# A long fused block: the merged rows split inside the last branch's panels, the convolution's low part three steps later

## The reference, cut to what matters

```
proj = h @ w_in
u_f, u_sc, u_qkv, z, b_logit, a_logit, gate_logit = split(proj)
y_f  = fourier_mix(u_f) @ w_fourier                      # branch 0
y_sc = short_conv_mix(u_sc, sconv_w) @ w_sconv_out       # branch 1: b * conv3(c * h)
y_dn = deltanet_branch(u_qkv, z, ...) @ w_dn_out         # branch 2: gated delta rule
merged = gates[0] * y_f + gates[1] * y_sc + gates[2] * y_dn
return merged @ w_out
```

## Time and profile before

| | |
|---|---|
| median of three runs | 1087.94 us |
| profiled execution, its own time | 1087.07 us |
| its span in the trace | 1085.3 us |
| mean granted TensorE clock | 0.97 of full |
| busy: TensorE, GpSimd, VectorE, ScalarE | 94%, 70%, 51%, 43% |

### The profile page before, as it was taken

One profiled execution on the slowest core, in us unless ns is written; L12 is line 12 of the kernel. 1 busy time (PEld: TensorE's weight loads), 2 busy tenths in 40 slices (PEclk: granted clock), 3 DMA queues, 4 the chain that ended last, 5 costly groups with the idle time before them and its releaser, 6 DMA issues.

```text
span 1085.3 us, 21538 instructions
## 1 busy us (share of the span) xinstructions
PE 1023.1 (94%) x8142; PEld 995.9 (92%) x8142; DVE 549.1 (51%) x1020; ACT 468.7 (43%) x698; POOL 762.6 (70%) x599
## 2 busy tenths in 40 slices
PE   7999999989899999998999899989999889999996
PEld 6899899989899999997898789989999879999995
DVE  4316994455444443335695463445654764445324
ACT  6243224454355444434546434423235364444441
POOL 2496666647859888996578734646629739999994
PEclk9999999999989999998999899989999889999998
DMA  9363333433526555664353122434225526656662
GB/s 351 106 194 117 117 117 117 136 98 117 194 82 184 173 181 159 181 178 152 117 169 107 57 62 94 120 115 126 90 79 172 188 69 194 193 179 185 178 182 70
DMA packets 48297, 154.60 MB, mean 142 GB/s; under 512 B 6028, under 2 KB 11156, under 8 KB 48232
## 3 DMA queue, kind: packets, MB, share of 16 engines
q1 hardware_dynamic: 46080, 151.31, 44.6%
q10 hardware_dynamic: 2152, 2.38, 0.6%
HBM read 151.57 MB, written 2.10 MB: 142 GB/s over the span
## 4 chain that ended last, share of the span: by engine, by line
PE 76%; DVE 12%; issue 4%; POOL 4%; ACT 3%; DMA 0%; SPq 0%; DVEq 0%; ACTq 0%; POOLq 0%
PE panel L1517 59%; PE panel L1561 3%; POOL wlo L591 2%; PE aux L1653 1%; PE panel L1604 1%; DVE qkv L1246 1%; DVE qkv L1251 1%; PE panel L1592 1%; DVE q L1154 1%; DVE s L1133 1%; DVE qkv L1242 1%; DVE k L1155 1%; PE aux L1875 1%; PE aux L1847 1%; PE aux L1838 1%
## 5 line engine op out<-in xcount | busy, mean ns | idle before, releaser
L591 POOL TENSOR_TENSOR wlo<-raw,whi 128x512 fp32r<-128x512 f32 x552 | 733.5, 1360 | 301.2 <-ACT whi L679 299.9
L1517 PE MATMUL panel<-xh,whi 128*128 128x256 f32 (+1 forms) x1504 | 443.5, 295 | 14.5 <-DVE xl L985 9.9
L1517 PE MATMUL panel<-xh,wlo 128*128 128x256 f32 (+1 forms) x1504 | 431.3, 287 | 0.0
L1517 PE MATMUL panel<-xl,whi 128*128 128x256 f32 (+1 forms) x1504 | 430.7, 286 | 0.0
L679 ACT ACTIVATE whi<-raw 128x1024 fp32r<-128x1024 f32 x276 | 286.5, 1053 | 175.0 <-PE panel L1517 152.2
L1517 PEld LDWEIGHTS panel<-xh,whi 128*128 128x128 f32 x1504 | 288.3, 192 | 19.3 <-issue 11.5
L1517 PEld LDWEIGHTS panel<-xl,whi 128*128 128x128 f32 x1504 | 287.4, 191 | 1.6
L1517 PEld LDWEIGHTS panel<-xh,wlo 128*128 128x128 f32 x1504 | 288.0, 191 | 0.0
L1517 PE MATMUL panel<-hh,whi 128*128 128x272 f32 (+1 forms) x352 | 100.1, 284 | 0.0
L1517 PE MATMUL panel<-hh,wlo 128*128 128x272 f32 (+1 forms) x352 | 99.9, 284 | 0.0
L1517 PE MATMUL panel<-hl,whi 128*128 128x272 f32 (+1 forms) x352 | 99.8, 284 | 0.0
(11 more groups left out here) (285 smaller groups left out, 1495.0 us busy)
## 6 DMA issues: line engine op xcount, KB each, us to landing
raw<-in_panels SPq DMA_DIRECT2D x228, 512.0 KB, 3.5
raw<-in_down SPq DMA_DIRECT2D x32, 448.0 KB, 3.3
raw<-in_down SPq DMA_DIRECT2D x16, 512.0 KB, 3.5
memk<-in_mem_panels SPq DMA_DIRECT2D x4, 512.0 KB, 7.4
memv<-in_mem_panels SPq DMA_DIRECT2D x4, 512.0 KB, 13.2
memx<-in_mem SPq DMA_DIRECT2D x4, 256.0 KB, 5.2
h<-in_x SPq DMA_DIRECT2D x1, 1024.0 KB, 8.0
spill<-h ACTq DMA_DIRECT2D x1, 1024.0 KB, 4.7
```

The costliest lines, as they stand in the source:

```text
L591: ins = nc.gpsimd.tensor_tensor(wlo[:, slot, half], raw[:, slot, half], whi[:, slot, half].bitcast(f32), ALU.subtract)
L1517: ins = M(bank[:, 0:w], wt[:, slot, P * t:P * t + P], x[:, kk, c0:c0 + w], start=first and m == 0 and n == 0, stop=last and m == len(pairs ...
```

## The change

Three things are changed. The merged rows get buffers of their own, `mgh` and `mgl`, in the space of `vt` and `kt` of the delta rule. Their high parts are made by ScalarE at the steps ("branch", 2, i), behind the wait for `mg_ready`, and their low parts by VectorE at the same steps, one tile behind (the last one after the loop). And a step ("sconv_low", t) three places behind ("sconv", t, 2) takes over VectorE's `yl`.

```diff
+    for i in range(4):
+        steps.insert(steps.index(("sconv", i, 2)) + 3, ("sconv_low", i))
     return steps
...
+        mgh = at("mgh", ar + 6528, [P, KT, ROWS], f32r)
+        mgl = at("mgl", ar + 8576, [P, KT, ROWS], f32r)
...
+                if kind == "branch" and step[1] == 2:
+                    act.wait_ge(mg_ready, 8 + i + 1)
+                    A(mgh[:, i, :], mg[:, i, :], ACT.Copy).then_inc(mg_high, 1)
...
             act.dma_start(h[:, :, META:LEN], a["spill"]).then_inc(h_back, 16)
-            out_wait(MIX_OUT[("gate", 2, 7)][0])
-            for kk in range(KT):
-                act.wait_ge(mg_ready, 8 + kk + 1)
-                if kk == 0:
-                    out_wait(MIX_OUT[("branch", 2, 7)][0])
-                A(xh[:, kk, 0:ROWS], mg[:, kk, :], ACT.Copy).then_inc(mg_high, 1)
...
+            def merged_low(kk):
+                dve.wait_ge(mg_high, kk + 1)
+                TT(mgl[:, kk, :], mg[:, kk, :], mgh[:, kk, :].bitcast(f32), ALU.subtract).then_inc(mg_low, 1)
...
                         TT(mg[:, i, :], mg[:, i, :], gt[:, g % 2, :], ALU.add).then_inc(mg_ready, 1)
+                        if step[1] == 2 and i:
+                            merged_low(i - 1)
...
                         TT(y, y, sc[:, t % 2, 0, META:LEN], ALU.mult).then_inc(yc_ready, 1)
-                        dve.wait_ge(y_high, 4 + t + 1)
-                        TT(yl[:, t, :], y, yh[:, t, :].bitcast(f32), ALU.subtract).then_inc(y_low, 1)
+                if kind == "sconv_low":
+                    dve.wait_ge(y_high, 4 + i + 1)
+                    TT(yl[:, i, :], cc[:, i % 2, 1, 0:ROWS], yh[:, i, :].bitcast(f32), ALU.subtract).then_inc(y_low, 1)
...
-            for kk in range(KT):
-                dve.wait_ge(mg_high, kk + 1)
-                TT(xl[:, kk, 0:ROWS], mg[:, kk, :], xh[:, kk, 0:ROWS].bitcast(f32), ALU.subtract).then_inc(mg_low, 1)
+            merged_low(KT - 1)
...
-                output(OUT2_O + i, OUT2_P + i, xh, xl, ROWS, each=(lambda kk: pe.wait_ge(mg_low, kk + 1)) if i == 0 else None)
+                output(OUT2_O + i, OUT2_P + i, mgh, mgl, ROWS, each=(lambda kk: pe.wait_ge(mg_low, kk + 1)) if i == 0 else None)
```

## The result

The changed kernel took 1079.74 us in the median of five runs (1078.5 to 1082.48), the kernel before 1087.07 in five (1086.77 to 1089.46): a ratio of 0.9936, 95% interval 0.9921 to 0.9951. A second comparison, 12 runs against 35, gave 1080.17 against 1085.83: 0.9949 (0.9935 to 0.9963), so 4 to 7 us. The forecast was 1081.3.

What follows compares the result with a forecast made beforehand. TensorE, busy 94% of the span, bounds the kernel, so only its stalls and slow-clock stretches can be won. Split 5.2 plus convolution 1.2 gives 6.4 us: 1080.7 for the profiled execution, 1081.3 taken, range 1079.2 to 1085.4.

Steps and rivals of the forecast that it cites:

- the prediction's own signs of being wrong: Granted clock 0.50 behind the output-pass stall, TensorE waiting for `wlo` between panels 194 and 203, or low parts over 2.3 us.
- The convolution's part: Delta rule: low part three steps later brings `aoff` earlier at two stalls, saving 0.45 and 0.75, together 1.2 us.
- The split: Mixer's end: merged rows split tile by tile inside the branch steps let the output panels start earlier, saving 5.2 us.
- low part 6 costs 0.41: Mixer's end: VectorE's low part of merged tile 6 takes 0.41 us, with GpSimd at the end of its queue.
- the two variants: The split saves 5.4 us, or 5.05 if longer `wlo` end GpSimd's queue 0.9 us later, about 847.1; 5.2 taken.
- Rival 1: Output passes: the clock falls again behind the shorter stall, 6.8 us at half speed costing 3.3 us; 1084.6 us, chance 0.26.
- Rival 2: Mixer's end: VectorE loses the port more than once, operations cost 2.68 us each; slower, 1089.5 to 1092.7 us, chance 0.06.
- What ScalarE's waits hold up: Branch steps: panel 200's weights' high part ends 2.0 to 4.2 us later, just hidden; nothing taken, up to 1 us lost.
- The sum: Whole kernel: 5.2 + 1.2 = 6.4 us saved, 1080.7 for the profiled execution; 1081.3 taken, chance 0.55.

Runs made afterwards that it cites:

- `aoff` ahead: The changed kernel with `aoff` of the second level's unit 1 made right behind unit 0, ahead of the convolution's five operations: 1072.89 us, ratio 0.9882 against before.
- split alone: Against the changed kernel, only the merged rows are split tile by tile; the convolution's low part stays in its step: 1082.28 us, ratio 0.9966 against before.
- convolution alone: Against the kernel before, only the convolution's low part is made three steps later; merged rows are split at the end: 1084.64 us, ratio 0.9994.
- the changed kernel's repeat: The changed kernel run and profiled once more with no edit: 1080.17 us, ratio 0.9949 against before.
- both edits: The changed kernel with unit 1's `aoff` made ahead of the convolution and the first two output passes interleaved: 1072.23 us, ratio 0.9877 against before.

## Why the prediction was right

*The place and the kind of gain.* Right. TensorE's stall behind the last branch matmul went from 3.5 us to 2.36 plus 0.18 (2.47 and 0.30 between starts, less one step each), and the time moved the way that was forecast. Not all of the mechanism came as forecast: one of the prediction's own signs of being wrong, a granted clock of 0.50 behind the stall, is there in the changed kernel's profile (844.8 to 848.2) and in its repeat. The other two, a wait for `wlo` and a low part of over 2.3 us, are not.

*The convolution's part.* Forecast 1.2 us (0.45 and 0.75). Measured 1.4 in delta. The first stall went from 4.24 to 3.33, the slow stretch behind it stayed 6.8 us, the second stall is gone; each as the steps had it. The other half of the statement, that the stall which stays costs 3.3 us and a slow stretch, was there to be read before, and `aoff` ahead shows that it was the larger prize.

*The split.* This is the term that was mis-sized: 5.2 us forecast, 4.4 measured in output where the clock stayed up (29.8 to 25.4), 3.0 to the norm's product in the changed kernel with a slow stretch. The step that failed is "low part 6 costs 0.41": I let GpSimd's queue end by 847.1 at the latest in before's time and took the middle between the two variants. The low parts had each lengthened a `wlo`, and the queue ended at 844.00 (in before's time 847.6): 1.4 us later than before, not 0.9. Of this 1.1 is longer `wlo`, and 0.3 the idle time in which GpSimd waited for panel 200's high part, a delay that I had checked against TensorE only. With 1.48 for low part 6 the same chain gives a stall of 2.7 us, against 2.54 measured. What happens at the norm differs from profile to profile: from the last output matmul to the norm's product it is 0.5 us before, 1.1 in the split alone (a wait of 0.8 for `sq`), but 0.4 in the changed kernel and 0.1 in `aoff` ahead. To the norm's product the split is thus worth 3.8 us in the split alone and 4.8 in `aoff` ahead; why was not followed up.

*Rival 1, the clock.* It got 0.26. A slow stretch came in two of the four profiles with this stall, but 3.4 us long, at 1.5 us, not the 3.3 that I had taken from the 6.8 us stretches. So the rival's time, 1084.6, was too dark, and its chance too low. Two of its premises fail. The stall was 2.36 us, longer than the 1.6 to 2.0 that I gave. And the border between stalls with and without a slow stretch was read from one execution: behind the same stall of 1.97 us for `yl` near 647, a stretch began at once in three of the twelve profiles (convolution alone, the changed kernel's repeat, both edits), and behind the one of 2.29 it was missing in two. The length of a stall alone does not decide it.

*Rival 2, the port lost twice.* Did not happen: no low part over 1.52 us. The long additions of the earlier trace rows came back at the same place in the changed kernel (2.16, 2.68 and 2.67 us near 747, 763 and 780), and none behind 800; why there and not here stayed open. The rival's times, 1089.5 to 1092.7, are 0.2 to 0.3 us off its own sum: 1087.07 + 3.3 - 1.2 is 1089.2, and 1092.5 with the slow stretch.

*What ScalarE's waits hold up.* The weights of panel 200: the high part ended at 835.86, in before's time 839.5, 3.6 us later than there (forecast 2.0 to 4.2). GpSimd was done at 838.50 and TensorE wanted the panel at 839.55: hidden by 1 us. TensorE waited for no `wlo` between panels 194 and 203. But the delay was not free, as GpSimd's queue ended 0.3 us later by it (above).

*The sum.* 1081.3 against 1079.74. The parts that I had counted gave 4.3 us in the first pair of profiles, less than the 6.4 forecast; 3.2 us came from slow stretches elsewhere that the change does not touch. So it was in part luck that the first comparison landed so near: the split gave less than forecast, and slow stretches that no term of the sum held gave more than the difference. The larger comparison, 5.5 us (4.0 to 7.1), holds both the forecast gain and the counted parts, and does not decide between them.

## What to carry to other kernels

Before taking an operation out of a queue in front of a stall, ask what else stands in that queue: here 0.9 us came from moving one operation back, and 5.6 from moving the awaited one in front of all. Work moved "beside" other work has another price there: VectorE's subtractions cost 1.5 us instead of 0.41 beside a busy GpSimd, and the operation that ends the chain pays it too, as long as GpSimd's queue runs. Under 0.5%, compare distances between two instructions in several profiles, not spans; a slow stretch inside a distance moved it here by 0.7 to 1.5 us.

## What the runs showed of the hardware

The slow-clock stretches differ from one execution to the next where the program does not: behind the same stall of 2.29 us near 238, in code that all these kernels share, the stretch was 6.8 us long in four of the twelve profiles, 3.4 in six, and missing in two; four had one of 3.4 near 113 and the others none. That fits the spread of 7 us over 35 runs of one kernel; whether it explains all of the spread was not tested.

A subtraction of VectorE with both operands in SBUF took 0.42 us with GpSimd idle and 1.51 with it busy; a product with one operand in PSUM took 0.42 in both. The Trainium skill (SBUF — State Buffer, section "Who interferes with whom") states that a VectorE instruction with two SBUF inputs contends with a GpSimd instruction that reads SBUF, and that one with at most one SBUF input, outside the 2-port modes, does not. These rows agree with it, and so do the squares: 0.97 us on average with both operands in SBUF, 0.42 with one in PSUM.
